# Moving the two halves of the down product and the weight spreading inside an expert block of a decoder-layer kernel

## The reference, cut to what matters

```python
logits = (xt @ p['w_router']) + p['b_router']
topv, topi = lax.top_k(logits, TOP_K)          # 4 of 32
wts = jax.nn.softmax(topv, axis=-1)
...
gu = xb @ p['w_gu'][e] + p['b_gu'][e]          # 1024 -> 2048
gate = jnp.minimum(gu[:, :D_FF], SWIGLU_LIMIT)
up = jnp.clip(gu[:, D_FF:], -SWIGLU_LIMIT, SWIGLU_LIMIT)
act = (up + 1.0) * gate * jax.nn.sigmoid(SWIGLU_ALPHA * gate)
y = (act @ p['w_down'][e] + p['b_down'][e]) * w[:, None]      # 1024 -> 1024
...
x = x + gt2 * moe(h, p)
```

## Time and profile before

| | |
|---|---|
| median of 3 runs | 1567.43 us (1558.92 to 1570.28) |
| time of the profiled execution | 1574.77 us |
| its span, first to last instruction | 1573.2 us |
| PE, busy share of the span | 85% |
| DVE, busy share | 43% |
| ACT, busy share | 13% |
| POOL, busy share | 12% |
| all transfers | 505.83 MB, 322 GB/s on average |

### The profile page before, as it was taken

How to read it: one execution, slowest core, us unless ns; L and a number is a source line. 1 busy time by engine, 2 the same in 40 slices (tenths; PEclk the granted TensorE clock), 3 DMA queues, 4 the chain that set the end, 5 groups by cost and what they waited for, 6 DMA issues and landing times.

```text
span 1573.2 us, 40569 instructions
## 1 busy us (share of the span) xinstructions
PE 1338.3 (85%) x16239; PEld 746.3 (47%) x16240; DVE 681.6 (43%) x1471; ACT 204.0 (13%) x463; POOL 191.5 (12%) x249
## 2 busy tenths in 40 slices
PE   5997989999998789979999696876949978869693
PEld 2455656367676545534555353433424434435352
DVE  2434656453635444534544343522523525325344
ACT  1124532311110210000000000000000000000001
POOL 2021310000000111111111111111111111120200
PEclk9999999988899899989999898987979979889797
DMA  9744992950093379699999999999999987996961
GB/s 353 264 170 137 349 397 105 345 193 1 12 324 151 134 302 417 276 424 422 425 425 425 429 428 427 429 429 428 415 428 418 415 346 332 425 428 286 414 271 63
DMA packets 63251, 505.83 MB, mean 322 GB/s; under 512 B 6528, under 2 KB 6648, under 8 KB 35332
## 3 DMA queue, kind: packets, MB, share of 16 engines
q1 hardware_dynamic: 55396, 480.98, 74.7%
q0 software_dynamic: 7808, 24.24, 4.6%
HBM read 500.09 MB, written 5.11 MB: 321 GB/s over the span
## 4 chain that ended last, share of the span: by engine, by line
PE 63%; DMA 15%; DVE 7%; issue 7%; POOL 3%; ACT 2%; SPq 2%; POOLq 0%; ACTq 0%; DVEq 0%
PE psum L558 59%; DMA ring<-in_w_gu 13%; POOL ring L2310 2%; DMA ring<-in_w_ada 2%; PE psum L727 2%; ACT region L1919 1%; DVE region L1837 1%; DVE region L1349 1%; SPq L2362 1%; DVE region L1194 1%; PE psum L759 0%; POOL region L2288 0%; DVE region L1817 0%; SPq L2387 0%; SPq L2388 0%
## 5 line engine op out<-in xcount | busy, mean ns | idle before, releaser
L558 PE MATMUL psum<-ring,region 128*32 128x256 f32 (+3 forms) x11328 | 724.6, 391 | 138.0 <-DMA ring<-in_w_gu 133.5
L558 PEld LDWEIGHTS psum<-ring,region 128*32 128x32 f32 (+2 forms) x11328 | 388.3, 114 | 443.2 <-DMA ring<-in_w_gu 154.5
L558 PE MATMUL psum<-region 32*128 32x320 f32 (+10 forms) x2714 | 252.9, 422 | 8.2 <-ACT region L1919 1.9
L2310 POOL COPY ring<-region 128x1024 f32<-128x1024 f32 x124 | 123.7, 1041 | 869.7 <-PE psum L558 869.7
L1817 DVE TENSOR_TENSOR region<-region,psum 128x1280 f32<-128x1280 f32 x110 | 161.3, 1467 | 119.4 <-PE psum L558 119.4
L1700 DVE TENSOR_SCALAR region<-psum,region 128x320 f32<-128x320 f32 x55 | 30.3, 551 | 346.9 <-PE psum L558 346.9
L1919 ACT ACTIVATE region<-psum 128x256 f32<-128x256 f32 (+7 forms) x164 | 72.6, 448 | 793.9 <-PE psum L558 697.6
L558 PE MATMUL psum<-region,ring 128*128 128x320 f32 (+1 forms) x640 | 174.0, 428 | 1.6 <-DVE region L1604 1.4
L558 PEld LDWEIGHTS psum<-region 128*32 128x32 f32 (+5 forms) x2714 | 102.8, 138 | 133.4 <-issue 91.4
L558 PEld LDWEIGHTS psum<-region,ring 128*128 128x128 f32 x640 | 119.6, 197 | 50.7 <-issue 8.4
L1686 DVE TENSOR_SCALAR region<-region 128x32 f32<-128x32 f32 x165 | 29.3, 238 | 85.6 <-issue 85.6
(11 more groups left out here) (335 smaller groups left out, 779.6 us busy)
## 6 DMA issues: line engine op xcount, KB each, us to landing
ring<-in_w_gu SPq DMA_DIRECT2D x128, 2048.0 KB, 12.1
ring<-in_w_down SPq DMA_DIRECT2D x33, 2048.0 KB, 10.5
region<-in_w_down SPq DMA_DIRECT2D x31, 2048.0 KB, 9.7
ring<-in_w_ada SPq DMA_DIRECT2D x12, 2048.0 KB, 14.2
ring<-in_w_in SPq DMA_DIRECT2D x11, 2048.0 KB, 20.2
ring<-in_cache_k SPq DMA_DIRECT2D x64, 256.0 KB, 5.4
ring<-in_cache_v POOLq DMA_DIRECT2D x64, 256.0 KB, 5.7
ring<-in_w_out SPq DMA_DIRECT2D x2, 2048.0 KB, 21.9
```

The lines of the kernel that those rows point to most:

```text
L558: return pe.matmul(out, lhsT, rhs, start=start, stop=stop, skip_group_check=True)
L2310: pool.tensor_copy(ring[:, moe_slot[n], part], landing[i][:, part])\
```

## The change

`down` is cut in its halves, which are called from different places of PE's block. Half 0 now comes behind quarter 0 and half 1 behind quarter 1. The weight spreading, which was behind the whole down product, is ahead of both. Each of the moved steps keeps its wait. The last expert's down product behind the loop keeps its order. No other engine's program is changed.

```diff
-            def down(expert):
-                for half in range(2):
-                    i = 4 + half
-                    if i in LANDED_APART:
-                        pe.wait_ge(piece_moved[LANDED_APART.index(i)], PIECES * expert + PIECES)
-                    else:
-                        pe.wait_ge(unit_landed[moe_slot[i]], 16 * expert + (landed_base[i] + 16))
-                    u = ring[:, moe_slot[i], :].rearrange("p (r f) -> p r f", r=4)
-                    for r in range(4):
-                        last = spread(B_Y, actT[:, 4 * half + r, :], lambda cols: u[:, r, cols],
-                                      half == 0 and r == 0, half == 1 and r == 3)
-                    last.then_inc(unit_read[i], 1)
+            def down_half(half, expert):
+                i = 4 + half
+                if i in LANDED_APART:
+                    pe.wait_ge(piece_moved[LANDED_APART.index(i)], PIECES * expert + PIECES)
+                else:
+                    pe.wait_ge(unit_landed[moe_slot[i]], 16 * expert + (landed_base[i] + 16))
+                u = ring[:, moe_slot[i], :].rearrange("p (r f) -> p r f", r=4)
+                for r in range(4):
+                    last = spread(B_Y, actT[:, 4 * half + r, :], lambda cols: u[:, r, cols],
+                                  half == 0 and r == 0, half == 1 and r == 3)
+                last.then_inc(unit_read[i], 1)
...
                 bias_rows()
                 gate_up_quarter(0, expert)
-                gate_up_quarter(1, expert)
-                pe.wait_ge(act_turned, b)
-                down(before_expert)
                 pe.wait_ge(weight_hot_ready, b)
                 spread_weights()
+                pe.wait_ge(act_turned, b)
+                down_half(0, before_expert)
+                gate_up_quarter(1, expert)
+                down_half(1, before_expert)
...
             pe.wait_ge(act_turned, blocks)
-            down(NE - 1)
+            down_half(0, NE - 1)
+            down_half(1, NE - 1)
```

## The result

| | before | with the change |
|---|---|---|
| median | 1567.43 us (1558.92 to 1570.88, 5 runs) | 1675.86 us (1675.05 to 1679.16, 5 runs) |
| ratio | | 1.0694, 95% interval 1.0655 to 1.0733 |
| span of the profiled execution | 1573.2 us | 1674.2 us |
| first to last block start of the loop | 948.84 us | 1049.88 us |

The change makes the kernel 7% slower. The forecast was 1669 us, in a range of 1638 to 1705. The last line places the loss: the loop over blocks is 101.0 us longer, the span as well.

What follows compares the result with a forecast made beforehand. Neither DMA nor PE was taken to bound the kernel alone: they are balanced and take turns. The terms +113 - 11 + 0 = +102 us, on the median of 1567.43, gave 1669 us, range 1638 to 1705.

Steps and rivals of the forecast that it cites:

- wait for `weight_hot`: PE behind quarter 0, ahead of the moved spreading: a new wait of 2.7 us in 42 blocks, +113 us.
- eleven waits for unit 0: PE's long waits for the next expert's first weights: ten shrink by 1.1 us each, -11 us.
- lower clock behind the new gaps: PE's matmuls behind the new waits: slowed in up to one block of five, 14 us in the range.
- half 0 in the pause behind unit 0: An expert's first block: half 0 fills PE's wait for unit 1, counted at 0, bounds -4 to +6 us.
- Where the wait comes from and how long it is: PE's early spreading: PE is there at 990.04, DVE's `weight_hot` is written at 992.69, so 2.7 us.
- The passing of the signal: From DVE's `weight_hot` to PE's spreading: 0.05 us, added to the 2.65 us wait.
- The count of 42: Of 54 loop blocks, eleven with long waits for unit 0 and the first are spared; 42 wait for `weight_hot`.
- That nothing takes the wait up: PE's and DVE's chains form a loop of 17.5 us a block against 14.76, with no idle time to absorb it.
- The give-back: One-block experts: refill issued 14.7 us behind block start, unit 0 lands 12.4 us later; long waits shrink, -11 us in all.
- B: Rival: DMA stays full and the waits for unit 0 absorb most added time; +56, 1623 us; chance 0.10, whole or part.
- C: Rival: PE's clock falls behind the new gaps, +71 us, 1740 us if in every block; chance 0.12 beyond one in five.
- Half 0 ahead of quarter 1 at nothing: First block of an expert: it ends by unit 3, so its 17.7 us stay; 0, bounds -4 to +6 us.

Runs made afterwards that it cites:

- e3: The changed kernel with the spreading behind half 0 instead of ahead of it: 1601.05 us, ratio 1.0155 to the kernel before.
- e4: The changed kernel with DVE writing `weight_hot` at the end of a block, for that block's own expert: 1586.38 us, ratio 1.0091 to the kernel before.
- e6_after_half_copy: The changed kernel with POOL copying only half of each piece of unit 5 (output not right): 1664.02 us, ratio 1.0599 to the kernel before.
- e5_before_hot_end: The kernel before, with DVE writing `weight_hot` at the end of its block: 1569.64 us, ratio 1.0005.
- e7_before_half_copy: The kernel before, with POOL copying only half of each piece of unit 5 (output not right): 1566.64 us, ratio 0.9967.
- e2_spread_only: Against the change, down product whole again behind quarter 1, spreading left behind quarter 0: 1677.20 us, ratio 1.0647 to the kernel before.
- e10_filled_gap: The changed kernel with 24 more small bf16 matmuls between quarter 0 and the wait for `weight_hot`: 1671.83 us, ratio 1.0631 to the kernel before.

## Why the prediction was right, point by point

The sum had +113 for the wait and -11 for the long waits. The loop got 101.0 us longer, and it is made up of these terms:

| term | predicted | measured |
|---|---|---|
| wait for `weight_hot` | 42 x 2.7 = +113 | 41 inside the stretch x (17.35 - 14.76) = +106 |
| eleven waits for unit 0 | -11 | 104.3 - 117.8 = -13.5 |
| lower clock behind the new gaps | 0 (up to 14 in the range) | 11 blocks, +18 |
| half 0 in the pause behind unit 0 | 0 (-4 to +6) | first blocks 197.8 us less 207.3, -9.5 |

The terms make 101.4; the remainder, -0.4 us, is the first block of the loop (1.2 us longer) and small differences in the others. (With the 42nd wait, in the last block, the first line is +109.)

- *Where the wait comes from and how long it is* was right: the rows of DVE gave 2.65 us, PE's idle time is 2.49 and the block is 2.59 us longer. So 2.7 was 0.1 us too much for a block, 4 us in all. The passing of the signal, 0.05 us in the prediction, is in the rows (1067.37 to 1067.43); what was sized too large is what follows the spreading, 12.69 us to the next block (1067.43 to 1080.12) where the prediction's terms give 12.83. The count of 42 was right.
- *That nothing takes the wait up* was right. The sum of both chains, 17.5 us a block, came out as 17.35. Moving either end of DVE's chain against PE's (e3, e4) moved the block by that much.
- *The give-back* was right in mechanism, and 2.5 us too small. The refill was issued 14.75 us behind the block's start (1000.95 to 1015.70; predicted 14.7), and 12.08 us later unit 0 was there (predicted 12.4). e6_after_half_copy shows that this chain sets the wait. The rival that the transfers take the wait in (B, 1623 us) fell.
- *The lower clock* (C) is real and was given too little weight: not in every block (+71), but in 11 of 42, +18. The forecast allowed for one block in five and 14 us, so its condition was in fact exceeded. The section on HAM oscillation of the page TensorE: Matmul & The Clock Gate in the Trainium skill describes such a fall. In its example the waits are of 3 to 5 us and the clock fell in every step; here gaps of 2.49 us, shorter than any of those, were enough in 11 cases and did no harm in 31. So the prediction stretched that example when it took from it that every block would lose.
- *Half 0 ahead of quarter 1 at nothing* is the step that failed: 0 with bounds of -4 to +6, and -9.5 measured. I took the end of the first block to be set by unit 3's landing. In the kernel before it was not, in any of the eleven: PE never waits for unit 3 there, and the 17.7 us are unit 1's landing and PE's own work. In four of them a slow stretch behind the pause therefore went onto the block in full. With half 0 in the pause it is gone, and only then does the block end by unit 3. Alone, the split makes the kernel 0.7% faster.

Against the profiled execution the sum was +102 and the span grew by 101.0, which is closer than its terms are, and that is luck: +18 and -9.5, both set to nothing, and the wait at +106 to +109 instead of +113 hide each other. Against the median it is 7 us off (108.4 measured), about the 7.3 us by which the profiled execution of before stood above its median. The prediction put the term on the median without asking where these 7.3 us come from. On other chips the median of before was 1570 to 1571, which would leave some 105 us. That execution had four long first blocks; that its shorter runs have fewer of them, which the change could then not save, was not seen, since they have no trace, and the two other profiles of such kernels do not settle it (four long ones at 1565.99 us in e5_before_hot_end, two at 1563.50 in e7_before_half_copy).

## What to carry to other kernels

Before a step is moved forward on one engine, look at when its operand is ready on the other engine, in the trace and not in the program: a wait with 2.6 us to spare becomes a wait of 2.6 us in each round when the step is moved by 5.3, and everything behind it in the queue pays. Write the length of a round as the sum of the two engines' pieces between their signals; that sum, 17.5 us here, gave the new period without a run. And when one change makes several moves, cost each by itself: here one move was worth 0.7% and the other cost 6.5%, and only a kernel with each alone shows it.

## What the runs showed of the hardware that was not expected

- Gaps of 2.49 us on PE, with full work before and behind, were followed by a stretch at the lower clock in 11, 13 and 15 of 42 blocks in three profiles (the change, e2_spread_only, e6_after_half_copy), 1.4 to 1.8 us each; gaps of 1.86 us in 8 of 42 (e10_filled_gap); gaps of 0.76 and 0.52 us in none (e3_behind_half0, e4_hot_at_end).
- A pause of 1.25 us right behind a first quarter that had run at the lower clock could keep the lower clock going: 10 of 33 first blocks lost 1.7 to 2.2 us more, and none of 99 in which PE had work for most of that pause (nine profiles); with work for half of it, 1 of 11 did (e2_spread_only).
